# The unit of the tokens' steps and index weights: tokens as the output rows, or features as the output rows and two transposes

## What is computed

```python
for l in range(DEPTH):                                   # DEPTH = 2
    h = rms_norm(x, norm1_g[l]) * (1.0 + sc1) + sh1      # 256 tokens x 1024
    proj = h @ w_in[l]
    q, k, v, iq, ik, iw, z, xbc, dt_raw, ga, gm = jnp.split(proj, SPLIT_POINTS, axis=-1)
    ...
    iq = apply_rope(iq.reshape(bsz, seq, IDX_HEADS, IDX_DIM), cos, sin)
    ik = apply_rope(ik[:, :, None, :], cos, sin)[:, :, 0, :]
    # score[t, s] = sum over 8 heads of iw[t, h] * relu(iq[t, h] . ik[s]); the best 64 keys are kept
    o_attn = dsa_attention(q, k, v, iq, ik, iw, n_keep) @ w_attn_o[l]
    ...
    dt = jax.nn.softplus(dt_raw.astype(jnp.float32) + dt_bias[l].astype(jnp.float32))
    a_cont = -jnp.exp(a_log[l].astype(jnp.float32))
    # dt (256 tokens x 32 heads) then steers the state-space scan
```

## Time and profile before

| what | value |
|---|---|
| median of 3 runs | 2376.15 us (2373.18 to 2376.77) |
| the profiled execution | 2371.44 us, span 2369.5 us |
| mean granted clock of TensorE | 0.983 |
| TensorE busy with matmuls | 2212.5 us, 93% of the span |
| VectorE busy | 1661.2 us, 70% |
| ScalarE busy | 1417.8 us, 60% |

### The profile page before, as it was taken

How to read it: one execution, slowest core, us unless ns; L and a number is a source line. 1 busy time by engine, 2 the same in 40 slices (tenths; PEclk the granted TensorE clock), 3 DMA queues, 4 the chain that set the end, 5 groups by cost and what they waited for, 6 DMA issues and landing times.

```text
span 2369.5 us, 42621 instructions
## 1 busy us (share of the span) xinstructions
PE 2212.5 (93%) x17568; PEld 2101.4 (89%) x17568; DVE 1661.2 (70%) x2998; ACT 1417.8 (60%) x2203; POOL 195.4 (8%) x178
## 2 busy tenths in 40 slices
PE   2989999999999999999899999899999989899999
PEld 2979899999998898999899987699999987799999
DVE  5898778678769887785997573647885563647653
ACT  3577887466546888854654556564553547564542
POOL 0000000022000000000330111000200111000000
PEclk9999999999999999999999999999999999999999
DMA  7455456567755554574455422245465323344554
GB/s 280 174 165 180 168 196 221 180 200 231 236 182 169 161 196 161 195 225 155 155 169 187 142 83 97 91 145 167 153 195 188 119 78 98 107 153 147 191 190 131
DMA packets 110593, 394.64 MB, mean 167 GB/s; under 512 B 12320, under 2 KB 13888, under 8 KB 110272
## 3 DMA queue, kind: packets, MB, share of 16 engines
q1 hardware_dynamic: 96768, 343.47, 44.3%
q0 software_dynamic: 11904, 43.03, 5.7%
q10 hardware_dynamic: 1728, 5.43, 0.6%
HBM read 390.83 MB, written 1.05 MB: 165 GB/s over the span
## 4 chain that ended last, share of the span: by engine, by line
PE 70%; DVE 14%; ACT 10%; issue 3%; DMA 1%; POOL 0%; SPq 0%; DVEq 0%; ACTq 0%
PE bank L547 69%; ACT scr L1033 4%; ACT WH L1033 3%; DVE WL L1534 3%; ACT L1022 2%; DVE arena L1598 2%; DMA ring<-in_w 1%; ACT arena L1033 1%; DVE scr L1598 1%; DVE arena L2217 1%; PE bank L627 1%; DVE scr L1581 1%; DVE scr L1787 1%; DVE arena L1712 1%; DVE scr L1774 0%
## 5 line engine op out<-in xcount | busy, mean ns | idle before, releaser
L1033 ACT ACTIVATE WH<-ring 128x1024 fp32r<-128x1024 f32 (+1 forms) x638 | 670.0, 1053 | 743.1 <-PE bank L547 719.5
L547 PE MATMUL bank<-HTH,WH 128*128 128x256 f32 x3392 | 979.0, 289 | 34.0 <-DVE scr L1598 13.6
L547 PE MATMUL bank<-HTL,WH 128*128 128x256 f32 x3392 | 961.7, 284 | 0.0
L547 PE MATMUL bank<-HTH,WL 128*128 128x256 f32 x3392 | 960.7, 283 | 0.0
L1534 DVE TENSOR_TENSOR WL<-ring,WH 128x1024 fp32r<-128x1024 f32 (+2 forms) x602 | 726.0, 1214 | 222.4 <-ACT WH L1033 220.7
L547 PEld LDWEIGHTS bank<-HTH,WH 128*128 128x128 f32 x3392 | 649.4, 191 | 49.2 <-issue 42.0
L547 PEld LDWEIGHTS bank<-HTL,WH 128*128 128x128 f32 x3392 | 649.1, 191 | 3.3 <-issue 3.0
L547 PEld LDWEIGHTS bank<-HTH,WL 128*128 128x128 f32 x3392 | 648.5, 191 | 0.0
L1022 ACT ACT_TABLE_LOAD x120 | 154.0, 1283 | 43.9 <-PE bank L547 26.7
L547 PE MATMUL bank<-ff2h,WH 128*128 128x256 f32 x512 | 144.0, 281 | 0.0
L547 PE MATMUL bank<-ff2h,WL 128*128 128x256 f32 x512 | 143.8, 281 | 0.0
(11 more groups left out here) (318 smaller groups left out, 3742.7 us busy)
## 6 DMA issues: line engine op xcount, KB each, us to landing
ring<-in_w SPq DMA_DIRECT2D x620, 512.0 KB, 4.0
arena<-in_wada POOLq DMA_DIRECT2D x80, 512.0 KB, 4.8
ring<-in_w SPq DMA_DIRECT2D x16, 384.0 KB, 4.3
arena<-in_wada SPq DMA_DIRECT2D x8, 512.0 KB, 19.6
arena<-in_wada ACTq DMA_DIRECT2D x8, 512.0 KB, 22.2
ring<-in_w SPq DMA_DIRECT2D x8, 288.0 KB, 2.8
XT<-in_xt SPq DMA_DIRECT2D x1, 1024.0 KB, 9.5
arena<-in_s POOLq DMA_DIRECT2D x4, 256.0 KB, 3.8
```

The costliest lines, as they stand in the source:

```text
L547: ins = e.matmul(out, a, b, start=(start and i == 0), stop=(stop and i == len(pairs) - 1))
L1033: return e.activation(out, a, func, **kw)
```

## The change

The `dt` unit becomes a "split" unit: the 40 weight columns are stationary and 256 tokens move, 8 chunks x 3 products = 24 matmuls. The output is then 40 rows (features) x 256 tokens, while its users want tokens as rows. So ScalarE copies the 40 x 256 block into `scr` 4 as soon as the unit is done, a new task `dt` at ticks 7 and 8 has TensorE turn it by two fp32 transposes into bank 6 (tick 7), and VectorE reads it from there (tick 8) with the same two operations as before. Bank 1 is now given back by ScalarE's copy and not by VectorE. The 128 x 320 weights, their transfer and their split into `WH` and `WL` stay the same. This happens in both layers.

```diff
--- before.py
+++ after.py
@@ -147,7 +147,7 @@
     w = "w_in"
     iq = groups_of("iq", l, w, 8, 3072, 4, "h")
     ik = [split_group("ik", l, 0, w, 8, [[(3584, 64), (3584, 64)]], "h")]
-    dt = [tokens_group("dt", l, 0, w, [(0, 8, [(3648, 8), (8776, 32)])], 64)]
+    dt = [split_group("dt", l, 0, w, 8, [[(3648, 8), (8776, 32)]], "h")]
     xc = [split_group("xc", l, o, w, 8, [[(5704 + 128 * (2 * o + j), 128)] for j in range(2)], "h")
           for o in (8, 10, 0, 1, 9, 11, 2, 3, 4, 5, 6, 7)]
     q = groups_of("q", l, w, 8, 0, 8, "h")
@@ -312,6 +312,7 @@
 
 
 A_TICKS = {
+    "dt": [7, 8],
     "attn0": [5, 7, 9, 11, 13, 15, 17, 19, 21, 23, 25, 27, 29, 31, 33, 35, 39, 41, 43, 45, 47, 51, 53, 55, 57, 59, 61,
               63, 65, 67, 69, 71],
     "attn1": [5, 7, 9, 11, 13, 15, 18, 20, 22, 24, 31, 33, 35, 37, 39, 41, 43, 45, 47, 49, 51, 55, 57, 59, 61, 63, 65,
@@ -470,7 +471,7 @@
         start_scalar, start_vector = sig("start_scalar"), sig("start_vector")
         out_done = sig("out_done")
 
-        FREED_BY_VECTOR = {"dt", "xc", "ao", "so", "res", "up", "pe", "b0", "b1", "b2"}
+        FREED_BY_VECTOR = {"xc", "ao", "so", "res", "up", "pe", "b0", "b1", "b2"}
 
         def bank_free(g):
@@ -635,6 +636,16 @@
                     mm(o[:, 0:T], [(v(h, 0), s[:, 0:T])], stop=False)
                     ins = mm(o[:, 128:T], [(v(h, 1), s[:, T:384])], start=False)
                 ins.then_inc(L.P.inc("pv", l, pr), 1)
+                yield
+
+            def steps(l):
+
+                p.wait_ge(ev_scalar("dt", l, 0, 2 * l))
+                for t in range(2):
+                    ins = e.transpose(LC.b[0][:, 64 * t:64 * t + 40], scr[0:40, 4, 128 * t:128 * t + 128],
+                                      con("id")[0:40, 0:40])
+                ins.then_inc(LC.P.inc("dt", l), 1)
+                yield
                 yield
 
             def ssd(l):
@@ -1082,6 +1093,8 @@
                     else:
                         ins = act(dst[:, :, 256 * gi:256 * gi + 256], v2(ps[:, :]), ACT.Copy)
                     ins.then_inc(ev_scalar.inc(k, l, gi, st), 1)
+                elif s == 0 and k == "dt":
+                    act(scr[0:40, 4, 0:T], ps[0:40, 0:T], ACT.Copy).then_inc(ev_scalar.inc(k, l, gi, st), 1)
                 elif s == 0 and k == "ik":
                     act(IK, ps[:, 0:T], ACT.Copy).then_inc(ev_scalar.inc(k, l, gi, st), 1)
                 elif s == 0 and k == "xc":
@@ -1474,7 +1487,11 @@
                 yield
                 yield
 
-            make = {"attn0": lambda l: attn(l, LA, 0), "attn1": lambda l: attn(l, LB, 1), "ssd": ssd,
+            def steps(l):
+                yield
+                yield
+
+            make = {"attn0": lambda l: attn(l, LA, 0), "attn1": lambda l: attn(l, LB, 1), "ssd": ssd, "dt": steps,
                     "gate0": lambda l: gate(l, 0), "gate1": lambda l: gate(l, 1), "gate2": lambda l: gate(l, 2),
                     "gate3": lambda l: gate(l, 3), "cuto": cuto, "gla": gla, "norms": norms,
                     "heads0": lambda l: heads(l, 0), "heads1": lambda l: heads(l, 1), "cutm": cutm, "s5": s5,
@@ -1610,13 +1627,7 @@
                 c2 = slice(2 * gi, 2 * gi + 2)
                 if s == 0:
                     p.wait_ge(unit_done(g.end))
-                if s == 0 and k == "dt":
-                    src = v2(ps[:, 0:128])
-                    p.wait_ge(in_rows("in"))
-                    e.tensor_copy(v2(small[:, 64:80]), src[:, :, 0:8])
-                    e.tensor_tensor(v2(dt), src[:, :, 8:40], twice(rows[:, 32 * l:32 * l + 32]), ALU.add).then_inc(
-                        ev_vector.inc(k, l, gi, st), 1)
-                elif s == 0 and k == "xc":
+                if s == 0 and k == "xc":
                     c = 2 * gi
                     conv("ssm_conv", 4, l, (c, c + 1), (XC[:, c, :], XC[:, c + 1, :]), ps,
                          [ev_scalar("conv", l, gi, 1)] * 2, g)
@@ -2212,6 +2223,15 @@
                                            ALU.subtract).then_inc(V.inc("yslo", l, j), 1)
                 yield
 
+            def steps(l):
+                yield
+                src = v2(LC.b[0][:, 0:128])
+                p.wait_ge(LC.P("dt", l), in_rows("in"))
+                e.tensor_copy(v2(small[:, 64:80]), src[:, :, 0:8])
+                e.tensor_tensor(v2(dt), src[:, :, 8:40], twice(rows[:, 32 * l:32 * l + 32]), ALU.add).then_inc(
+                    ev_vector.inc("dt", l, 0, 2 * l), 1)
+                yield
+
             def ada(l, j, tile, ready):
                 p.wait_ge(ready, start_scalar("c"))
                 e.tensor_tensor_reduce(tile, tile, silc, 1.0, 0.0, ALU.mult, ALU.add, mod[:, l, j:j + 1]).then_inc(
...
```

## The result

| | before | changed |
|---|---|---|
| median | 2376.39 us (4 runs, 2373.18 to 2376.77) | 2361.36 us (4 runs, 2356.54 to 2362.91) |
| profiled execution | 2371.44 us, span 2369.5 | 2359.89 us, span 2358.0 |
| TensorE busy | 2212.5 us | 2199.9 us |
| VectorE busy | 1661.2 us | 1666.3 us |
| mean granted clock | 0.983 | 0.987 |

The ratio is 0.9947 (95% interval 0.9927 to 0.9968). Forecast was 2364 us, 12.3 us less; the medians lie 15.0 apart, the two profiled executions 11.55. A second measurement, 5 runs of the changed kernel against 18 of the kernel before, gave 0.9949 (0.9937 to 0.9962), which is 12.1 us of 2373.16, and is the better figure.

What follows compares the result with a forecast made beforehand. TensorE bounds the kernel (70% of the chain), slowed by the `dt` unit and its clock fall. 13.16 us saved less 0.44 for transposes and 0.44 for VectorE: 2376.15 - 12.3 = 2363.9 us, range 2359 to 2370.

Steps and rivals of the forecast that it cites:

- The chain: Chain that ended last: TensorE unbroken from 54.98 us for 26.68 us, so a microsecond saved there before 81.7 reaches the end.
- The sum: Both layers: 13.16 us saved on TensorE, 0.44 us added for transposes and 0.44 us for VectorE, 12.3 us less.
- The unit: Unit 5 (`dt`): 24 matmuls at 0.118 us take 3.14 us, saving 4.58 us in layer 0, 4.29 us in layer 1.
- rival B: Unit 5: few stationary columns slow the rounded matmuls to plain fp32 pace, 0.46 us each; 2379.6 us; chance 0.03.
- C: Time saved on TensorE misses the end, through ScalarE's late copy at tick 7 or transfers; 2374 to 2377 us; chance 0.03.
- The clock: From unit 6 to unit 7's second matmul: full clock stays up, saving 2.78 us in layer 0, 1.51 us in layer 1.
- A: In or after the new unit: 40 of 128 array columns are too little, clock falls; 2367 to 2370.5 us; chance 0.11.
- D: Around unit 5: the clock's fall has another cause than the unit's shape and stays; 4.2 us saved, 2372 us; chance 0.03.
- The row with 64 stationary columns: Profile run of plain fp32 matmuls at 1455.64, clock 1.00; nearest evidence that the clock stays up with 40 columns.
- The transposes: Two on TensorE ahead of the turn of `ik`: 0.22 us a layer added, bounds 0 and 0.4.
- The copy's cover: ScalarE's copy is done at 69.7, TensorE reaches tick 7 at 70.9: cover 1.2 us, so no wait.
- the main case: Forecast for the whole kernel: 12.3 us less, 2363.9 us, spanning 2359 to 2368; chance 0.80.

## Why the prediction was right

- **The chain.** It ran through TensorE at the place, and time taken there arrived: 7.16 us at `hi` of unit 11 in layer 0 (82.06 - 64.89 = 17.17 before, 10.01 after), 5.29 in layer 1 (15.29 and 10.00). The sum had 7.14 and 5.58.
- **The unit.** 3.14 us forecast, 3.22 measured. The step was right (0.118, 0.117), which rules out rival B; TensorE never stood idle for ScalarE's copy, which rules out C. The first step was taken from a matmul with 40 moving columns, 0.43 us, and is 0.52 for 256: 0.09 us a layer too little.
- **The clock.** It stays at 1.00, so neither A nor D came. That the narrow run brought the fall is shown, not only argued: the same 48 matmuls made wide keep the clock, the same 48 narrow ones spread out keep it, 24 narrow in a row can lose it, 72 wide ones with 40 stationary columns do not. What keeping the clock was worth is at least 7.3 us of 12.15 in the stretches. The row with 64 stationary columns was a sound neighbour for 40.
- **The transposes.** 0.22 us forecast, 0.43 measured (1.10 - 0.67), just over the upper bound of 0.4. The price was taken from 128 x 128 transposes, and the 40 x 40 form is dearer by as much again.
- **VectorE.** 0.22 us in the chain, measured 0.22, and shown by moving it away. The copy's cover held: 1.2 us forecast, 1.3 measured (69.3, 70.64). No wait for a transfer shows in the rows of these units.
- **The sum.** TensorE's part comes to 6.85 + 5.30 = 12.15 us where 13.16 - 0.44 = 12.72 stood: 0.18 from the first steps, 0.42 from the transposes, less 0.03 of rounding. Less VectorE's 0.44 that is 11.7. Layer 0 gained 0.31 us more at `hi` of unit 11 than TensorE's stretch shows: it came 3.29 us behind the second matmul of unit 7 before, in all three executions (3.28, 3.28), and 2.98 after. The chain view puts 0.35 us ahead of that `hi` down to "issue" before, time in which ScalarE waited for nothing that the profile shows, and 0.04 after. It is not the clock: the three variants of the kernel before that kept 1.00 up to there or had it back by unit 7 have the delay too, in layer 0 alone (3.29, 3.31 and 3.28 us with 48 wide, 48 spread and 24 narrow matmuls), and every variant of the changed kernel is without it (2.97 to 2.99). So it goes with the program and not with the stretch; what it is stays open. 12.0 us in all, against 11.55 between the spans and 12.1 from the larger measurement. That these agree so well with 12.3 is in part luck: two terms were too small by 0.6 us together, the 0.31 us that nobody forecast made up for half of it, and behind layer 1 the lead wanders by several microseconds before it ends at 11.5. The absolute time was less close, 2364 against 2361.4 and 2360.4, because the three runs it was counted from (2376.15) lie 3 us above the median of 18.
- **Where I was too wide.** I gave the main case a spread because two layers lost unlike amounts and I took that for chance. It is not: 13.88 and 12.32 us repeat to 0.01 us. The spread that is real lies elsewhere: of the 6.1 us between the first and the third execution of the kernel before, 3.0 are there at the start of unit 5 and come from the program's start; the rest arises behind the two layers of this block, where low stretches of the clock lie at unlike places.
- **The page.** The Trainium skill, "TensorE: Matmul & The Clock Gate", section "HAM oscillation — how this bites in real kernels", ties the fall to idle gaps. The trace does not agree here: TensorE was busy for all of each window in which it fell, and 256 moving columns in the same places cured it. The rows decide: the clock can fall without an idle gap in the profile. "Busy" needs care, though. The profile models the ends of matmuls and gives a narrow one 0.27 us although the next starts 0.112 us later, so it does not show how much of its time the array had columns moving through it.

## What to carry to other kernels

Look at the granted clock behind a run of narrow matmuls, not only at the run: here 48 matmuls with 40 moving columns cost more through the half clock they left to themselves and the next unit (7.3 us in two layers) than through their number. Put the wide side of a product on the moving side, or spread the narrow matmuls among wide ones, and even padding the moving side with columns that nobody reads paid for itself (0.997). When you price a small operation, take a row of the same shape: both terms that were off here came from rows with another width.

## What the runs showed of the hardware

- A 40 x 40 fp32 transpose pair between other matmuls costs 0.43 us, a 128 x 128 pair 0.22 us. The smaller form is the slower one, and part of the price is paid by the matmul behind it.
- Behind the fp32 turn of `iq`, which moves 512 columns, the first matmul starts its successor after 0.43 us if 40 columns move and after 0.52 to 0.53 us if 256 do, whether 40 or 128 columns are stationary. Behind the turn of `ik`, which moves 256, it is 0.30 us with 256 moving.
- TensorE's clock fell to half while the profile had the engine busy for 4.00 of 4.00 us, under a run of matmuls with 40 moving columns, and stayed low for about 10.2 us in layer 0 and 6.8 us in layer 1. This and the time of the stretch repeat over three executions, the latter to 0.01 us, while some other low stretches of the same program come and go.
